# A hybrid decoder layer on one Trainium2 core: 64-row and 16-token matmuls placed side by side on row and column tiles

## The reference

```python
n = rms_norm(h)
u = n @ w_in                       # every mixer's columns and the three gates
y_a = rwkv7_time_mix(...)          # 6 heads x 64 = 384 channels
y_b = stick_breaking_attention(..) # 5 heads x 64 = 320 channels
y_c = forgetting_attention(..)     # 5 heads x 64 = 320 channels
merged = (g[:, :, 0] * (y_a @ w_p_rwkv)
          + g[:, :, 1] * (y_b @ w_p_sb)
          + g[:, :, 2] * (y_c @ w_p_fox))
h = h + merged @ w_out
h = h + hierarchical_moe(rms_norm(h))   # 16 experts, 2 for each token
return h[:, 16:]
```

## Time and profile before

| what | value |
|---|---|
| time, median of 3 runs | 1141.86 us (1141.19 to 1764.89) |
| the profiled execution's own time | 1134.54 us |
| its span in the trace | 1132.8 us |
| PE busy | 1013.8 us, 89% |
| DVE busy | 314.3 us, 28% |
| ACT busy | 246.2 us, 22% |
| granted TensorE clock, mean of the span | 0.951 |

### The profile page before, as it was taken

The page is one execution under the profiler, slowest core; times in us unless marked ns, Lnnn a source line. Parts: engine busy times, 40 slices in busy tenths (PEclk is TensorE's granted clock), DMA queues, the critical chain, the costliest instruction groups (busy, mean ns, idle before and its releaser), DMA issues.

```text
span 1132.8 us, 15398 instructions
## 1 busy us (share of the span) xinstructions
PE 1013.8 (89%) x6388; PEld 599.4 (53%) x6388; DVE 314.3 (28%) x665; ACT 246.2 (22%) x475; POOL 83.6 (7%) x196
## 2 busy tenths in 40 slices
PE   0998898998998867899999999999999759999992
PEld 0886677876766643455554444443335434444441
DVE  1122363223223134611111333323421251212110
ACT  4201531121121275532330000042012200111100
POOL 7700000000000000000000000000000011121211
PEclk9999799999999968999999999999999869999997
DMA  6222003011000100131111101025371346999994
GB/s 170 67 75 75 0 1 76 5 46 49 2 2 2 50 9 0 45 87 38 38 37 32 39 24 37 20 59 182 99 249 41 136 155 207 335 352 340 359 286 112
DMA packets 104262, 111.52 MB, mean 98 GB/s; under 512 B 16305, under 2 KB 93233, under 8 KB 104129
## 3 DMA queue, kind: packets, MB, share of 16 engines
q1 hardware_dynamic: 99584, 93.76, 25.8%
q0 software_dynamic: 4608, 16.78, 5.8%
HBM read 97.40 MB, written 15.20 MB: 99 GB/s over the span
## 4 chain that ended last, share of the span: by engine, by line
PE 83%; DVE 5%; ACT 4%; issue 4%; DMA 2%; SPq 0%; POOL 0%; DVEq 0%; POOLq 0%; ACTq 0%
PE ps L1321 14%; PE ps L1536 9%; PE ps L1223 8%; PE ps L1169 6%; PE ps L1150 6%; PE ps L1463 6%; PE ps L1493 5%; PE ps L1550 5%; PE ps L1174 4%; PE ps L1389 2%; PE ps L1422 1%; PE ps L1423 1%; ACT L501 1%; PE ps L1528 1%; PE ps L1448 1%
## 5 line engine op out<-in xcount | busy, mean ns | idle before, releaser
L1321 PE MATMUL ps<-arena 128*128 128x512 f32 x384 | 183.0, 617 | 1.0 <-ACT yT_all L604 0.3
L1321 PEld LDWEIGHTS ps<-arena 128*128 128x128 f32 x384 | 70.6, 195 | 72.5 <-issue 71.1
L1223 PE MATMUL ps<-arena 64*64 64x64 f32 x2376 | 82.5, 223 | 12.6 <-DVE arena L829 10.8
L1223 PEld LDWEIGHTS ps<-arena 64*64 64x64 f32 x2376 | 75.4, 137 | 33.5 <-issue 25.6
L1169 PE MATMUL ps<-arena 128*128 128x264 f32 x320 | 84.9, 410 | 0.2 <-ACT arena L538 0.2
L1536 PE MATMUL ps<-arena 128*128 128x512 f32 x176 | 78.9, 600 | 1.5 <-issue 1.3
L458 POOL DMA_INDIRECT arena<-n_rows,idx x16 | 15.7, 979 | 868.2 <-DVE idx L1035 860.3
L1150 PE MATMUL ps<-arena 128*128 128x264 f32 x320 | 72.5, 386 | 1.9 <-PE ps L1150 1.2
L1463 PE MATMUL ps<-yT_all,arena 128*128 128x512 f32 x144 | 68.0, 614 | 0.0
L1150 PEld LDWEIGHTS ps<-arena 128*128 128x128 f32 x320 | 60.0, 189 | 14.1 <-issue 2.8
L1169 PEld LDWEIGHTS ps<-arena 128*128 128x128 f32 x320 | 59.8, 196 | 13.1 <-issue 1.2
(11 more groups left out here) (318 smaller groups left out, 1139.4 us busy)
## 6 DMA issues: line engine op xcount, KB each, us to landing
arena<-in_moe_w_down SPq DMA_DIRECT2D x16, 1024.0 KB, 12.9
arena<-in_w_in SPq DMA_DIRECT2D x24, 512.0 KB, 3.9
arena<-in_moe_w_gate SPq DMA_DIRECT2D x11, 1024.0 KB, 14.4
arena<-in_moe_w_up SPq DMA_DIRECT2D x11, 1024.0 KB, 17.1
arena<-in_w_in SPq DMA_DIRECT2D x9, 1024.0 KB, 5.4
yT_all<-in_moe_w_gate SPq DMA_DIRECT2D x5, 1024.0 KB, 14.6
yT_all<-in_moe_w_up SPq DMA_DIRECT2D x5, 1024.0 KB, 16.9
arena<-in_w_out SPq DMA_DIRECT2D x1, 4096.0 KB, 13.5
```

Of the source, the lines that this page charges most:

```text
L1223: ins = mm(psf[q, 512 * bank + c * CH:512 * bank + (c + 1) * CH], lhs(q, c), rhs(q, c), start=True, stop=True)
L1321: ins = mm(ps[:, 5 + 2 * (n % 2), :], gate_w[:, (n + 1) % 4, c, :], nT[:, c, META:L], start=(c == 0), stop=(c == DC - 1))
```

## The change

First, the values. The groups of full token tiles stay, eight of them (4 tiles by 2 halves). The 16-token tile's two groups become one last group, "tail". Each of its eight channel chunks is two steps: a matmul of 16 tokens by the first half's 320 columns into PSUM partitions 0 to 15, and one by the second half's 325 into partitions 32 to 47 of the same bank, so on another column tile. The number of steps stays 240 (`STEPS`). ACT empties the tail with three copies in place of one for a first-half and two for a second-half group.

Second, the projection. A round does the seven full-row chunks of its three branches first, each branch in its own bank of six (0, 1, 2, 3, 4, 6), and then the two 64-row chunks in halves of 256 tokens: branch 1, branch 2, branch 1, branch 2, which alternate between rows 0 to 63 and rows 64 to 127 and write two different banks. The semaphore counts of branches 1 and 2 come with their last halves.

```diff
-        groups = [... "q" ...] + [(N_SHIFT + 5 + f // 5, "v", f // 5, f % 5) for f in range(10)]
+        groups = [... "q" ...] + [(N_SHIFT + 5 + f // 4, "v", f // 4, f % 4) for f in range(8)]
+        groups += [(N_SHIFT + 6, "tail", 0, 4)]
         NF = len(groups)
+        STEPS = (NF + 1) * DC
...
-                else:
-                    r = KT[i][1]
-                    if j == 0:
-                        done(a.activation(V[0:r, i, 0:SW], ps[0:r, b, 0:SW], ACT.Copy), "fill_out")
-                    else:
-                        done(a.activation(V[0:r, i, SW:], ps[0:r, b, 0:SW], ACT.Copy))
-                        done(a.activation(flog[0:r, i, :], ps[0:r, b, SW:SW + FH], ACT.Copy), "fill_out")
+                elif kind == "v":
...
+                else:
+                    done(a.activation(V[0:16, i, 0:SW], ps[0:16, b, 0:SW], ACT.Copy))
+                    done(a.activation(V[0:16, i, SW:], ps[32:48, b, 0:SW], ACT.Copy))
+                    done(a.activation(flog[0:16, i, :], ps[32:48, b, SW:SW + FH], ACT.Copy), "fill_out")
...
-                while out_n[0] < NF and DC * (out_n[0] + 1) <= issued[key]:
+                while out_n[0] < NF and (DC * (out_n[0] + 1) if out_n[0] < NF - 1 else STEPS) <= issued[key]:
...
-                    done(tt(dst, gate(n), ps[:, 2 + n % 2, :], ALU.mult), "proj_used")
+                    done(tt(dst, gate(n), ps[:, (0, 1, 2, 3, 4, 6)[n % 6], :], ALU.mult), "proj_used")
...
+                        if kind == "tail":
+                            k0, r = KT[k]
+                            mm(ps[0:r, b, 0:SW], nT[:, c, k0:k0 + r], slot(i - 1)[:, c, 0:SW], start=(c == 0), stop=(c == DC - 1))
+                            yield
+                            ins = mm(ps[32:32 + r, b, 0:RING_W], nT[:, c, k0:k0 + r], w[:, c, 0:RING_W], start=(c == 0), stop=(c == DC - 1))
...
+                bank = lambda b: (0, 1, 2, 3, 4, 6)[(n + b) % 6]
                 for b in range(3):
-                    if n >= 2:
-                        pe.wait_ge(sem("proj_used"), n - 1)
-                    for c in range(3):
-                        rs = slice(0, P) if b == 0 or c < 2 else slice(64 * (b - 1), 64 * b)
-                        ins = mm(ps[:, 2 + n % 2, :], wpr[rs, dc % 2, 3 * b + c, :], yT[b][rs, c, :], start=(c == 0), stop=(c == 2))
-                    ins.then_inc(sem("proj_psum"), 1)
-                    n += 1
+                    if n + b >= 6:
+                        pe.wait_ge(sem("proj_used"), n + b - 5)
+                    for c in range(3 if b == 0 else 2):
+                        ins = mm(ps[:, bank(b), :], wpr[:, dc % 2, 3 * b + c, :], yT[b][:, c, :], start=(c == 0), stop=(b == 0 and c == 2), skip_group_check=(b > 0))
+                    if b == 0:
+                        ins.then_inc(sem("proj_psum"), 1)
+                for k in range(2):
+                    for b in (1, 2):
+                        rs = slice(64 * (b - 1), 64 * b)
+                        cols = slice(256 * k, 256 * k + 256)
+                        ins = mm(ps[:, bank(b), cols], wpr[rs, dc % 2, 3 * b + 2, :], yT[b][rs, 2, cols], start=False, stop=True, skip_group_check=True)
+                        if k == 1:
+                            ins.then_inc(sem("proj_psum"), 1)
+                n += 3
```

More of the change, by code:

```diff
@@ L240, in slot_sem @@
             return sem(f"ring{i % RING}" if i < N_RING else f"late{(i - N_RING) % 2}")
-        groups = [(N_SHIFT + f // 4, "q", f // 2, f % 2) for f in range(20)] + [(N_SHIFT + 5 + f // 5, "v", f // 5, f % 5) for f in range(10)]
+        groups = [(N_SHIFT + f // 4, "q", f // 2, f % 2) for f in range(20)] + [(N_SHIFT + 5 + f // 4, "v", f // 4, f % 4) for f in range(8)]
+        groups += [(N_SHIFT + 6, "tail", 0, 4)]
         NF = len(groups)
+        STEPS = (NF + 1) * DC
         pe_order = []
@@ L256, in hybrid_layer @@
         for key, n_ in pe_order:
-            issued[key] = min(filled, NF * DC)
+            issued[key] = filled
             filled += n_
-        assert filled - 6 >= NF * DC, filled
+        assert filled - 6 >= STEPS, filled
         def qchunk(kind, i, part):
@@ L541, in group_out @@
                         done(a.activation(dst[64:128], ps[64:128, b, 0:HALF], ACT.Copy), "fill_out")
-                else:
-                    r = KT[i][1]
-                    if j == 0:
-                        done(a.activation(V[0:r, i, 0:SW], ps[0:r, b, 0:SW], ACT.Copy), "fill_out")
-                    else:
-                        done(a.activation(V[0:r, i, SW:], ps[0:r, b, 0:SW], ACT.Copy))
-                        done(a.activation(flog[0:r, i, :], ps[0:r, b, SW:SW + FH], ACT.Copy), "fill_out")
+                elif kind == "v":
+                    if j == 0:
+                        done(a.activation(V[:, i, 0:SW], ps[:, b, 0:SW], ACT.Copy), "fill_out")
+                    else:
+                        done(a.activation(V[:, i, SW:], ps[:, b, 0:SW], ACT.Copy))
+                        done(a.activation(flog[:, i, :], ps[:, b, SW:SW + FH], ACT.Copy), "fill_out")
+                else:
+                    done(a.activation(V[0:16, i, 0:SW], ps[0:16, b, 0:SW], ACT.Copy))
+                    done(a.activation(V[0:16, i, SW:], ps[32:48, b, 0:SW], ACT.Copy))
+                    done(a.activation(flog[0:16, i, :], ps[32:48, b, SW:SW + FH], ACT.Copy), "fill_out")
             def groups_out(key):
-                while out_n[0] < NF and DC * (out_n[0] + 1) <= issued[key]:
+                while out_n[0] < NF and (DC * (out_n[0] + 1) if out_n[0] < NF - 1 else STEPS) <= issued[key]:
                     group_out()
@@ L1167, in qkv_products @@
                     for c in range(DC):
-                        if kind == "q":
+                        if kind == "tail":
[3 more added lines that the diff above has]
+                            ins = mm(ps[32:32 + r, b, 0:RING_W], nT[:, c, k0:k0 + r], w[:, c, 0:RING_W], start=(c == 0), stop=(c == DC - 1))
+                        elif kind == "q":
                             ins = mm(ps[:, b, 0:HALF], w[:, c, (j % 2) * P:(j % 2 + 1) * P], nT[:, c, k * HALF:(k + 1) * HALF],
@@ L1280, in _ @@
                 if p == RC - 1:
-                    fill_qkv(NF * DC)
+                    fill_qkv(STEPS)
                     pe.wait_ge(sem("fill_out"), NF)
```

## The result

The changed kernel takes 1130.4 us, the median of 16 runs (1129.0 to 1131.4), against 1135.1 us for 15 runs of the kernel before (1132.7 to 1142.1). By the medians it is 4.7 us; the two figures differ because the kernel before comes in two groups, eight executions at 1132.7 to 1135.1 us and seven at 1139.4 to 1142.1. The profiled executions, of which that of before is in the lower group, differ by less: spans of 1129.3 and 1132.8 us.

A forecast was written before the change was run, and what follows sets the result against it. TensorE bounds the kernel, busy 89% of the span. Terms -10.0 + 1.45 + 1.6 + 0.6 - 3.8 + 0.46 = -9.7 us, taken off the 1141.9 us median, give 1132.2 us; range 1125 to 1139.

The forecast's parts named there:

- The projection: Branch projection: a round takes 7.26 us against 8.51; eight rounds give -10.0 us.
- Row tiles run at once, in their own order: Projection's 64-row matmuls: both row tiles overlap fully, against the skill's program-order rule; four 256-column records per tile take 0.86 us.
- the rival of strict order: Projection and column pairs: overlap only between neighbours, starts keeping program order; +2.5 us in the projection, 1135.7 us; chance 0.1.
- The reading of line 1195: Trace's near pair: eight 264-column records on two row tiles took 2.14 us, read as full overlap.
- The wait at the end: End of projection: two more VectorE operations before the output projection, +1.45 us, a wait of 3.05 us.
- Its clock: Behind the projection's last wait: granted clock falls to 0.50, +1.6 us as likelier case, 0 as other bound.
- The value products: Value products: +0.6 us second pair's wider steps, -3.8 us third pair's overlapping column tiles, +0.46 us second small ScalarE copy.
- The bound that no row gave: Third pair's value products: -3.8 us if two column tiles over the same 128 rows overlap, 0 if not.
- Hidden weights, free banks: Projection: third round's weights arrive in time, else up to 1 us once; six banks in rotation cost nothing.
- About two other stretches of 1.6 us at half clock that may come or go as the program shifts: Elsewhere in the program: a part of the forecast's own range, 1127 to 1135 us, with no term in the sum.

The follow-up runs named there:

- one_row_tile: Changed kernel with branch 2's 64-row halves also on rows 0 to 63, using branch 1's third chunk as operands: 1136.3 us.
- whole_chunks: Changed kernel with the two 64-row chunks as whole matmuls of 512 tokens, branch 1's then branch 2's, not alternating halves: 1130.8 us.
- narrow_first: Changed kernel with the 64-row halves at the head of each projection round instead of its end: 1129.3 us.
- one_column_tile: Changed kernel with both matmuls of a tail step pair writing partitions 0 to 15, the same column tile: 1134.1 us.
- values_only: Kernel before with the value part of the change alone: 1137.7 us, ratio 1.0015.
- filled_waits: Changed kernel with three extra 512-column matmuls in PE's two waits around the cumulated forget gates: 1127.7 us.
- proj_filled: Kernel before with the projection part alone plus three extra matmuls in PE's two waits around the cumulated forget gates: 1128.0 us.
- empty_early: Changed kernel with ScalarE emptying the tail group right behind its copy of AKV, not behind that of W2: 1123.7 us, ratio 0.9877.

## Why the prediction was right

The forecast was 1132.2 us in a range of 1125 to 1139; measured were 1130.4. That the time came so close is in part luck. The 1141.9 us that it started from was the median of three executions, two of them from the upper group of the kernel before. From the median of the 15 the same sum gives 1125.4 us, 5 us too low. The start was 6.8 us too high, and the gain was smaller than forecast: 9.7 us against 6.0 by the ratio and 4.7 by the medians. The steps of the sum, though, came as worked out:

- *The projection*, -10.0 us, a round of 7.26: measured 7.27 a round. With the longer wait the stage came out at -8.5 us, forecast -10.0 + 1.45 = -8.55. `one_row_tile` splits the -10.0 into 6.9 us of overlap and 3.0 us of fewer changes of row count.
- *Row tiles run at once, in their own order*: shown by `whole_chunks`, and the rival of strict order (+2.5 us) is out. The reading of line 1195 carried it.
- *The wait at the end*, 3.05 us: measured 3.05. *Its clock*, +1.6 us: measured +1.7. `narrow_first` ties both to the bunched multiplies.
- *The value products*: +0.6, -3.8 and +0.46 make -2.74 us; the third recurrence came 2.77 us earlier, and from the second to the third it takes 2.8 us less. The bound that no row gave, two column tiles over the same rows, is settled by `one_column_tile` at 3.6 us of 3.8.
- *Hidden weights, free banks*: as forecast, no wait.

The step that failed is a term the sum did not have. "About two other stretches of 1.6 us at half clock that may come or go as the program shifts" was put into the range, either way, with zero in the sum. In the profiled executions it was +6.4 us, net four such stretches. In the timed runs it was 3.6: -2.8 - 8.5 + 1.7 is -9.6 us, and -6.0 were measured by the ratio, against runs of before of which some have the same stretches. At a mean clock of 0.940 to 0.942 the kernel before took 1140.3 to 1142.6 us and the changed one 1129.0 to 1131.3, 11 us less; the changed kernel is at 0.937 to 0.944 in every execution. That a step of -2.8 us can be worth nothing in the end (`values_only` against before, `filled_waits` against `proj_filled`) was not in any rival; that the projection part alone, 1126.9 us, is faster than both parts together follows from it.

What stays open is why the kernel before escapes these stretches in most of its executions and the changed kernel in none of 16. The runs show that load in the two waits removes the stretch in the first head, and that a recurrence that starts 0.9 us sooner (`empty_early`) goes with its absence too and with other changes behind. They don't separate place from load, and the recurrence's own half clock, by which the traces already differ ahead of the two waits, was not tried.

## What to carry to other kernels

Ragged chunks of 64 rows cost a whole matmul each plus a change of row count on either side, 0.19 us a change here; gathered and put on both row tiles, they cost half, and no alternation by hand is needed. Whoever gathers them should ask what completes together at the end, and put the ragged ones first, so that the last piece to finish is a whole one with little behind it. Time each part of a change alone: here one of two parts, each of whose steps came out as forecast, took back time from the other. And where PE waits 1 to 3 us between dense stages, a gain ahead of the wait is only kept if the clock holds: compare granted clocks of single executions before believing in a change of a few microseconds, and try a few idle matmuls in the wait.

## What the runs showed of the hardware

Two row tiles of 64 rows ran four records of 512 columns in 1.13 us, the same whether the two tiles alternate in program order or one stands whole ahead of the other (`whole_chunks`); one tile needs 1.99 us for the same columns. Two column tiles over the same 128 rows overlapped fully, starts 0.01 us apart, weight loads included. PE's clock stayed at 1.00 behind a wait of 1.61 us and went to 0.50 behind waits of 2.62 and 3.05 us. Behind the waits of 1.65 and 1.40 us, which lie close together, it held in two traces and fell in seven, with the waits as long in all of them. Three matmuls in these waits, 2.6 us of work that is thrown away, made the whole kernel 2.7 us faster.
